# Taking the first two chunks of a down projection together, row block by row block

## The reference

```
def conv_ffn(xn, w_up, cw, cb, w_down):
    a = xn @ w_up                                   # 1024 -> 2 * 2816
    T = a.shape[1]
    ap = jnp.pad(a, ((0, 0), (CONV_W - 1, 0), (0, 0)))
    a = sum(ap[:, j:j + T] * cw[j] for j in range(CONV_W)) + cb
    gate, val = jnp.split(a, 2, axis=-1)
    return (jax.nn.gelu(gate, approximate=True) * val) @ w_down   # 2816 -> 1024
```

## Time and profile before

| what | value |
|---|---|
| median of three runs | 2685.9 us |
| lowest, highest | 2664.63, 2690.1 us |
| profiled execution, its own time | 2680.04 us |
| its span, first to last instruction | 2678.3 us |
| mean granted TensorE clock | 0.919 of full |
| TensorE busy | 2370.1 us, 88% |
| VectorE busy | 1396.6 us, 52% |
| GpSimd busy | 1105.2 us, 41% |
| ScalarE busy | 591.2 us, 22% |

### The profile page before, as it was taken

One profiled execution on the slowest core, in us unless ns is written; L12 is line 12 of the kernel. 1 busy time (PEld: TensorE's weight loads), 2 busy tenths in 40 slices (PEclk: granted clock), 3 DMA queues, 4 the chain that ended last, 5 costly groups with the idle time before them and its releaser, 6 DMA issues.

```text
span 2678.3 us, 34115 instructions
## 1 busy us (share of the span) xinstructions
PE 2370.1 (88%) x14068; PEld 1899.8 (71%) x14068; DVE 1396.6 (52%) x2005; ACT 591.2 (22%) x1159; POOL 1105.2 (41%) x632
## 2 busy tenths in 40 slices
PE   7998799999699996999996989658688796899998
PEld 5866588887477774888883567547488785688886
DVE  5455557446733346465566531677945464550431
ACT  2052220121232322210211300302533321210110
POOL 4613367666342222667662103503210024456663
PEclk9999899999799998999997999868888877999999
DMA  4201134335121111334345001102110001222321
GB/s 154 95 24 48 45 97 173 103 110 184 49 71 40 46 34 39 104 133 149 95 163 203 24 16 49 63 1 77 34 49 3 2 1 55 65 93 95 105 93 63
DMA packets 54058, 204.12 MB, mean 76 GB/s; under 512 B 6000, under 2 KB 6128, under 8 KB 52880
## 3 DMA queue, kind: packets, MB, share of 16 engines
q1 hardware_dynamic: 52560, 188.34, 21.5%
q0 software_dynamic: 1344, 13.60, 1.3%
HBM read 197.72 MB, written 4.19 MB: 75 GB/s over the span
## 4 chain that ended last, share of the span: by engine, by line
PE 81%; DVE 14%; ACT 3%; issue 1%; POOL 1%; DMA 0%; DVEq 0%; SPq 0%; POOLq 0%; ACTq 0%
PE bank L493 59%; PE bank L781 3%; PE bank L809 2%; PE bank L610 1%; DVE nb L619 1%; PE bank L1339 1%; PE bank L1359 1%; PE bank L796 1%; PE bank L2020 1%; PE bank L1367 1%; PE bank L2005 1%; DVE nb L1911 1%; PE bank L2262 1%; PE bank L2016 1%; PE bank L785 1%
## 5 line engine op out<-in xcount | busy, mean ns | idle before, releaser
L493 PE MATMUL bank<-xn_r,parts_r 128*128 128x512 f32 (+1 forms) x3104 | 979.5, 394 | 48.5 <-DVE big_r L504 13.2
L493 PE MATMUL bank<-big_r,parts_r 128*128 128x512 f32 x3112 | 900.5, 393 | 1.0 <-POOL parts_r L484 1.0
L482 POOL TENSOR_SCALAR parts_r<-ring 128x1024 fp32r<-128x1024 f32 x297 | 337.4, 1136 | 1193.8 <-PE bank L493 1169.3
L484 POOL TENSOR_TENSOR parts_r<-ring,parts_r 128x1024 fp32r<-128x1024 f32 x297 | 743.2, 2503 | 24.7
L493 PEld LDWEIGHTS bank<-xn_r,parts_r 128*128 128x128 f32 x3104 | 591.9, 193 | 176.4 <-issue 41.6
L493 PEld LDWEIGHTS bank<-big_r,parts_r 128*128 128x128 f32 x3112 | 584.7, 189 | 123.7 <-DVE big_r L504 2.7
L740 DVE SCALAR_TENSOR_TENSOR big<-bank,small,big 128x511 f32<-128x511 f32 x88 | 65.9, 749 | 277.1 <-ACT big L719 277.1
L719 ACT ACTIVATE big<-bank,small 128x512 f32<-128x512 f32 x88 | 68.3, 781 | 497.1 <-PE bank L493 497.1
L2403 DVE TENSOR_TENSOR big<-big 128x512 f32<-128x512 f32 x32 | 82.3, 2573 | 69.9 <-ACT big_r L2384 69.9
L2357 DVE SCALAR_TENSOR_TENSOR h<-bank,vecs,h 128x512 f32<-128x512 f32 x24 | 17.8, 750 | 193.3 <-PE bank L493 193.3
L493 PE MATMUL bank<-parts_r,xn_r 128*128 128x384 f32 x352 | 95.3, 353 | 15.5 <-DVE big L1902 9.6
(11 more groups left out here) (349 smaller groups left out, 2985.4 us busy)
## 6 DMA issues: line engine op xcount, KB each, us to landing
ring<-weights SPq DMA_DIRECT2D x297, 512.0 KB, 3.5
cst<-mod_w SPq DMA_DIRECT2D x48, 512.0 KB, 4.0
big<-consts POOLq DMA_DIRECT2D x1, 4096.0 KB, 16.1
cst<-consts SPq DMA_DIRECT2D x2, 1280.0 KB, 8.4
h<-x SPq DMA_DIRECT2D x8, 256.0 KB, 5.4
h_store<-h POOLq DMA_DIRECT2D x1, 2048.0 KB, 7.7
h<-h_store POOLq DMA_DIRECT2D x1, 2048.0 KB, 8.9
out<-mix SPq DMA_DIRECT2D x8, 256.0 KB, 2.2
```

The costliest lines, as they stand in the source:

```text
L482: pool.tensor_scalar(rounded(w_hi[:, slot]), w, 1.0, 0.0, ALU.mult, ALU.add).then_inc(sem("hi_ready"), 1)
L484: pool.tensor_tensor(rounded(w_lo[:, slot]), w, value(w_hi[:, slot]), ALU.subtract).then_inc(part_ready, 1)
L493: mm = pe.matmul(ps, rounded(w[a]), rounded(x[b]), start=(start and n == 0), stop=(stop and n == 2))
```

## The change

`lead` becomes 2 where the input becomes ready tile by tile and kt is 11, which is true of the four down projections alone. For each of the 11 row blocks TensorE then does chunk 0 and chunk 1, and after that chunks 2 to 7 as before. The banks of both are taken ahead of the first product.

Chunk 1 begins in the middle of unit 1, so a second condition makes TensorE take that unit when it first touches it. And since the products are no longer issued in the order of the blocks, the count for `product_done` is worked out from the last chunk that a unit's eight blocks reach, in place of the chunk of the product that was issued last.

```
-                if j == 0:
+                if j == 0 or (f and f < lead and k == 0):
                     take(pe, u)
...
-                product_done[u] = after(full, full0 + f + 1)
+                product_done[u] = after(full, full0 + min(((u - u0) * 8 + 7) // kt, chunks - 1) + 1)
...
-            lead = min(PARTS, chunks) if ready and kt == KD else 1
+            lead = min(PARTS, chunks) if ready and kt == KD else 2 if ready and kt == KH else 1
```

## The result

The changed kernel takes 2717.5 us at the median of four runs (2709.8 to 2722.4); the kernel before, with one more run beside them, 2675.5 us (2664.6 to 2690.1). The ratio worked out from these runs is 1.014, 95% interval 1.0094 to 1.0187 (the two medians alone, 41.9 us apart, would give 1.016). Timed again, it was 1.013 (1.0093 to 1.0167). The change makes the kernel slower, by 1.3 to 1.4%; both intervals lie clear of one, with their lower ends just under 1%.

What follows compares the result with a forecast made beforehand. TensorE, busy 88% of the span and holding 81% of the end-setting chain, bounds it. 4 x (2.60 - 0.36 + 2.74) = 19.9 us plus 8.0 of clock gives 2708 us, 2713 as median; range 2698 to 2724.

Steps and rivals of the forecast that it cites:

- Gain: Last input tile of each down projection: needed 60 matmuls after the start, not 30, so its wait goes, -0.36 us a projection.
- Wait 1: Start of each down projection: bank 1, freed by VectorE's second convolution step, is awaited before the first matmul, 2.60 us delay.
- Wait 2: Fourth weight unit of each down projection: its slot frees only when chunk 0 completes at matmul 63, 2.74 us delay.
- The lower bound: Least delay from the late fourth weight unit, with GpSimd's two passes as fast as alone (3.49 us): 1.84 us.
- Moved, costed at nothing: Down projections: units 1 and 2 due sooner, VectorE's copy, modulation products and SyncE's loads 9 us later, all at no cost.
- rival E: SyncE's modulation loads, 9 us later, are not made up and a ring unit behind them is late: 2722 us; 6%.
- Clock: TensorE after the eight new stops: five followed by half clock, 1.6 us each, 8.0 us together.
- Rival A: Down projections: both waits, and the slow clock after five or more stops, 2713 to 2719 us; 46%.
- B: Down projections: both waits, but the clock falls after four stops or fewer, 2706 to 2712 us; 32%.
- C: Down projections: one wait not paid in full, 2702 us, or 2695 with the fourth unit's wait gone altogether; 12%.
- D: Down projections: no delay, bank 1 free and unit 3 in time, only the 1.4 us gain left, 2684 us; 4%.

## Why the prediction was right, step by step

2713 us was predicted, 2717.5 measured, in the range 2698 to 2724; slower by over 1% had the larger chance, and came, though the intervals reach down to 0.9%. That the two medians agree within 5 us is in part luck. The prediction put the changed median 27.1 us above the median of before, and the two lie 41.9 us apart; but before's moved from 2685.9 down to 2675.5 with its fourth run. Against the change of 27.9 us, the ratios of 1.013 and 1.014 are 35 to 38 us, with 25 to 50 inside the intervals.

- *Gain*, 0.36 us a projection: right. The waits on line 504 are gone.
- *Wait 1*, 2.60 us, a stop of 2.43: right in all four, 2.48 us. It stands alone with the banks alone, and goes when bank 1 is asked for later.
- *Wait 2*, 2.74 us, a stop of 2.57: 2.49 to 2.50 us. GpSimd's passes took 4.31 us (433.46 to 437.77) where I took 4.39. The lower bound was real too: beside an idle VectorE they took 3.49 us and the stop was 1.67, a delay of 1.83 where the bound said 1.84. What I read as a pass merely lengthened by line 1196 is a pass that waited. The changed kernel's VectorE in that place, two instructions of line 1196, and one more that GpSimd left alone:

```profile
433.94 1.64 DVE L1196 SCALAR_TENSOR_TENSOR big<-cst,vecs,big 128x1024 f32<-128x1024 f32 x1
...
435.50 3.35 DVE L1196 SCALAR_TENSOR_TENSOR big<-cst,vecs,big 128x1024 f32<-128x1024 f32 x1
...
444.68 1.27 DVE L1196 SCALAR_TENSOR_TENSOR big<-cst,vecs,big 128x1024 f32<-128x1024 f32 x1
```

The first product ends at 435.58; GpSimd's second pass, sent off at 434.59, ends at 437.77, just its 2.36 us of lone time and 0.8 more; and VectorE's next product, 1.27 us long beside an idle GpSimd, ends 1.1 us after that. The two take turns. The rule of the Trainium skill ("SBUF — State Buffer", section "Who interferes with whom") is that the later of the two blocks until the first has finished its instruction, and these rows agree with it within 0.2 us: what the pass pays is the rest of the instruction that it meets, 0.8 us here, where 1.0 us of it was left.

- *Moved, costed at nothing*: wrong in one place. Unit 5 was late by 0.8 us in each first half, where before it was late by 0.1. I had its split at up to 5.36 us, but used that only to say when GpSimd would come to unit 6, and never set it against when unit 5 is needed. Its slot comes free when chunk 2 ends, with matmul 99, and it is needed by matmul 121, about 4.6 us later at full clock. Before, its split took 4.37 us (438.78 to 443.15) and all but fitted; now it took 2.05 + 3.22 us, 5.35 to the end:

```profile
446.01 2.05 POOL L482 TENSOR_SCALAR parts_r<-ring 128x1024 fp32r<-128x1024 f32 x1 [2.94 <-PE bank L493]
448.14 3.22 POOL L484 TENSOR_TENSOR parts_r<-ring,parts_r 128x1024 fp32r<-128x1024 f32 x1
```

  The products that I had moved by 9 us were then in full run beside it. I followed them to the weight loads and the banks, and not to the engine that takes turns with VectorE. It is worth about 1.6 us. The rest of the step held: no unit came late behind SyncE's modulation loads (rival E), and VectorE had caught up by chunk 7.
- *Clock*: the mechanism was right, the size low. I let five of eight stops be followed by a fall at 1.6 us each; six and eight were, in two profiles. In all profiles with such stops (2.48 to 2.51 us) 25 of 36 were. Filling the stops gave 10 us back, against 8.0 predicted.

The sum of the terms as measured, 4 x (2.64 - 0.36 + 2.66) + 1.6 + 10 = 31.4 us (2.64 and 2.66: the stops and the 0.16 by which matmuls overlap), stands to the 30.2 and 30.9 us read off the profiles. The ratios' centre is some 5 us above that; with intervals of 10 us and more to either side, whether anything else costs stays open.

Rival A happened. B needed fewer falls. C and D fell with the two stops standing in all four places.

## What to carry to other kernels

Before reordering work so that an input is needed later, look up how long it is waited for: here 0.36 us, and the price was two waits of 2.5 us. Interleaving chunks moves every release tied to a complete chunk (a bank, a weight slot) to the end of the group, while the next need comes just as early; count the matmuls between the two. Interleave only as far as the late tiles ask for, and then finish the chunks one after another: that alone made this kernel 0.7% faster.

## What the runs showed of the hardware that was not expected

A stop of TensorE of about 2.5 us costs up to 1.7 us more than itself: around the end of 25 of 36 such stops the granted clock fell to 0.50 for 3.4 us. How often differs by profile: eight of eight in one, none of four in another. Behind the four stops of 1.67 us of one profile it never fell, which is too few to tell. With ten useless matmuls in each stop it stayed at 1.00 in all eight places.

VectorE and GpSimd took turns where line 1196 met line 484: GpSimd's pass of 2.36 us took 3.18, and VectorE's product of 1.27 us took 3.35.

One kernel, profiled twice, spent 83.9 and 69.1 us on the same 640 matmuls of the recurrence, at a mean granted clock of 0.66 and 0.83. A difference of 10 us between two single profiles of this kernel is no evidence unless it lies where the edit does.
